# Prompt attention of a hybrid decoder step: where a step's products with the values stand in TensorE's order

## The reference, cut to what matters

```python
s = jnp.einsum('...qgrd,...kgd->...qgrk', q, k).astype(jnp.float32) * SCALE
p = jax.nn.softmax(jnp.where(mask, s, NEG), axis=-1)
o_win = jnp.einsum('...qgrk,...kgd->...qgrd', p.astype(v.dtype), v)   # o_sel, o_cmp alike
o = gates[..., 0:1] * o_cmp + gates[..., 1:2] * o_sel + gates[..., 2:3] * o_win
```

## Time and profile before

| | us |
|---|---|
| runs | 1827.85, 1829.54, 1830.10 (median 1829.54) |
| the profiled execution's own time | 1826.82 |
| its span, first to last instruction | 1825.2 |
| the attention stage's matmuls in it | from 648.3 to 948.5 |
| mean granted TensorE clock | 0.978 |

### The profile page before, as it was taken

The page is one execution under the profiler, slowest core; times in us unless marked ns, Lnnn a source line. Parts: engine busy times, 40 slices in busy tenths (PEclk is TensorE's granted clock), DMA queues, the critical chain, the costliest instruction groups (busy, mean ns, idle before and its releaser), DMA issues. The chain is left out here.

```text
span 1825.2 us, 29596 instructions
## 1 busy us (share of the span) xinstructions
PE 1713.0 (94%) x11664; PEld 1511.1 (83%) x11664; DVE 838.9 (46%) x1606; ACT 618.1 (34%) x1188; POOL 148.9 (8%) x261
## 2 busy tenths in 40 slices
PE   5999999995999779999989999999999999999997
PEld 4989988994864655555549889999999999999997
DVE  5556342131116366677775675322332233223476
ACT  5222322210010156666655554202320232023343
POOL 1000000013534300000000110000000000000011
PEclk9999999997999799999999999999999999999999
DMA  8111011144966500000017533211111111111365
GB/s 292 47 48 48 24 48 42 47 104 116 239 180 190 153 17 1 1 1 1 1 45 198 174 119 93 66 47 47 47 47 47 47 47 47 47 47 47 110 177 166
DMA packets 215500, 148.98 MB, mean 82 GB/s; under 512 B 13565, under 2 KB 204882, under 8 KB 214978
## 3 DMA queue, kind: packets, MB, share of 16 engines
q1 hardware_dynamic: 180050, 99.38, 19.4%
q0 software_dynamic: 12848, 37.47, 6.7%
q10 hardware_dynamic: 22464, 10.23, 2.2%
HBM read 134.76 MB, written 16.47 MB: 83 GB/s over the span
## 5 line engine op out<-in xcount | busy, mean ns | idle before, releaser
L2077 PE MATMUL psum<-act_hi,whi 128*128 128x344 f32 x960 | 310.2, 323 | 8.6 <-DVE wlo L2196 5.6
L2077 PE MATMUL psum<-act_lo,whi 128*128 128x344 f32 x960 | 307.4, 320 | 0.0
L2077 PE MATMUL psum<-act_hi,wlo 128*128 128x344 f32 x960 | 307.4, 320 | 0.0
L2196 DVE TENSOR_TENSOR wlo<-wraw,whi 128x1024 fp32r<-128x1024 f32 x111 | 136.0, 1225 | 253.7 <-ACT whi L2093 253.5
L2077 PE MATMUL psum<-hidden_hi,whi 128*128 128x344 f32 x768 | 246.4, 321 | 0.0
L2077 PE MATMUL psum<-hidden_hi,wlo 128*128 128x344 f32 x768 | 245.3, 319 | 0.0
L2077 PE MATMUL psum<-hidden_lo,whi 128*128 128x344 f32 x768 | 245.2, 319 | 0.0
L2093 ACT ACTIVATE whi<-wraw 128x1024 fp32r<-128x1024 f32 x111 | 117.4, 1057 | 338.1 <-PE psum L2077 332.0
L231 PE MATMUL psum<-act_hi,whi 128*128 128x344 f32 x648 | 214.8, 331 | 4.1 <-DVE act_lo L404 4.1
L231 PE MATMUL psum<-act_hi,wlo 128*128 128x344 f32 x648 | 208.1, 321 | 0.0
L231 PE MATMUL psum<-act_lo,whi 128*128 128x344 f32 x648 | 208.1, 321 | 0.0
(11 more groups left out here) (366 smaller groups left out, 2474.7 us busy)
## 6 DMA issues: line engine op xcount, KB each, us to landing
wraw<-in_w_down SPq DMA_DIRECT2D x48, 512.0 KB, 3.7
wraw<-in_w_up SPq DMA_DIRECT2D x40, 512.0 KB, 4.1
wraw<-in_w_in SPq DMA_DIRECT2D x27, 512.0 KB, 3.8
wraw<-in_w_o SPq DMA_DIRECT2D x23, 512.0 KB, 4.6
h_features<-mixed_then_h POOLq DMA_DIRECT2D x24, 172.0 KB, 2.5
h_again<-h_features POOLq DMA_DIRECT2D x24, 172.0 KB, 3.0
x_rows<-in_x_prompt SPq DMA_DIRECT2D x4, 1024.0 KB, 9.2
dec_pages<-in_cache_sel_k SPq DMA_DIRECT2D x64, 64.0 KB, 3.0
```

The lines of the kernel that those rows point to most:

```text
L2077: last = pe.matmul(ps[:, u % 3, 0:TN], wt[:, kt, :], xt[:, kt, cols], start=(kt == 0 and i == 0), stop=(kt == KT - 1 and i == 2))
L2196: dve.tensor_tensor(m.wlo[p % 2][:], wraw[raw_slot[p]][:], m.whi[p % 2][:].bitcast(F32), ALU.subtract).then_inc(lo_ready, 1)
```

## The change

In TensorE's loop `output` moves from the end of an iteration, behind `other_keys(k)`, to a place between `sel_keys(k)` and `turn(k-2)`, one iteration later: part x of a group is issued in the iteration after the one that had it before. The loop has one more iteration for it. On VectorE `add_halves` moves by one iteration too. No operation is added or left out, and ScalarE's list is untouched.

```diff
             pe.wait_ge(casts, 1)
-            for k in range(len(steps) + 6):
+            for k in range(len(steps) + 7):
                 if k < len(steps):
                     sel_keys(k)
+                if k >= R + 3:
+                    output((k - 3) // R - 1, (k - 3) % R)
                 if 2 <= k < len(steps) + 2:
                     turn(k - 2)
                 if k < len(steps):
                     other_keys(k)
-
-                if k >= R + 2:
-                    output((k - 2) // R - 1, (k - 2) % R)
@@ VectorE
-                if k % R == 2 and k >= 2 * R + 2:
+                if k % R == 3 and k >= 2 * R + 3:
                     add_halves(k // R - 2)
```

## The result

The changed kernel takes 1866.03 us (median of four runs, 1865.36 to 1867.41) against 1828.88 us before: a ratio of 1.0206, 95% interval [1.0193, 1.0219]. It is slower by 37 us. The profiled execution took 1865.63 us.

The account below looks back on a forecast made before the run. TensorE's own list was taken to bound the attention stage; 35.3 us of new waits for the selected exponential less 4.2 us of vanishing waits gave net +31 us on 1829.5, so 1860.5 us, range 1848 to 1873 (86%).

Parts of the forecast that it names:

- TensorE's list bounds the stage, and the products hide ScalarE's chain: Attention stage: TensorE's own work bounds it; 1.87 us of products cover ScalarE's copies and selected exponential, leaving 1.08 us spare.
- The sum of c - b, 35.3 us: Attention steps: c (first transpose to accumulator read plus 0.06) less b (to window scores' end), where positive: 35.3 us wait.
- What goes, 4.2 us: Attention stage: TensorE's existing waits for exponentials, mostly in the short steps at the end, vanish: 4.2 us taken off.
- Products followed by transposes cost the same as products followed by scores: TensorE's list in 56 attention steps: same 1.87 us price for eight instructions, with 6 us either way.
- I cost the clock at nothing: Attention stage: TensorE's granted clock stays at 1.00 throughout despite the new waits, adding 0 us.
- Nothing moves: Rival 1, TensorE's list: its work is the whole bound, so the exchange is free; 1829.5 us, 4%.
- Faster: Rival 2, attention stage: products cover VectorE's selected maximum, 4.2 us of waits vanish without a new one; 1825.3 us, 3%.
- VectorE's halves: Rival 3: query split and halves share an iteration, seven steps lose up to 2.1 us each; 1876 us, 5%.
- The falling clock: Rival 4, attention stage: a quarter of its 260 us at 1.2 GHz adds 65 us; some 1925 us, 2%.

Follow-up runs that it names:

- second comparison: The changed kernel run again without any edit, for a second profile: 1869.94 us, 1.0242 of the kernel before.
- only_after_r0: Kernel before, moving only the products that stood behind steps with r = 0 to behind the next step's selected scores: 1826.58 us, 1.0004.
- exp_first: Changed kernel with ScalarE's selected exponential of step k put ahead of the copies of step k-2: 1845.26 us, 1.0112 of the kernel before.
- vector_part_undone: Changed kernel with VectorE's add_halves put back at k % 4 = 2: 1872.33 us, 1.0244 of the kernel before.
- only_after_r123: Kernel before, moving only the products that stood behind steps with r = 1, 2, 3; those behind r = 0 stay: 1873.09 us, 1.0237.
- exp_before_last_copy: Changed kernel with ScalarE's selected exponential ahead of only the last copy of step k-2 and the compressed copy: 1835.11 us, 1.0037 of the kernel before.
- before_exp_first: Kernel before, products unmoved, with ScalarE's selected exponential put ahead of the copies of step k-2: 1891.44 us, 1.0344.
- between_turn_and_scores: Kernel before with the products moved behind the transposes, ahead of the same iteration's window scores: 1860.59 us, 1.0186.
- before_exp_before_last_copy: Kernel before, products unmoved, with ScalarE's selected exponential ahead of the last copy of the step two back: 1826.73 us, 0.9995.

## Why the prediction was right, and what it missed

The direction, the main mechanism and the range were right: 1866.0 us for 1860.5 (1848 to 1873). Against the median of before it is +37 us for +31, and +43 in the second comparison; in the profiled steps +42 for +31. The largest term was right, two terms put at nothing weren't.

- *TensorE's list bounds the stage, and the products hide ScalarE's chain.* Right. The run `only_after_r0` shows that a product costs nothing where the chain is hidden otherwise, and `exp_first` that the wait for the exponential disappears if it isn't behind the copies.
- *The sum of c - b, 35.3 us.* Measured waits: 32.4 us in 43 steps (the forecast says "some 42"; its own list by blocks counts 43). In step 11 the wait was 0.78 us for 0.85. The sum went by the distance between two starts, and a wait is counted from the end of the last matmul: from the start of the window scores to the next selected scores step 11 takes 1.92 us instead of 1.08, a difference of 0.84. With some 0.07 us more for each wait, the 32.4 us are about 35.5, just what was forecast.
- *What goes, 4.2 us.* Right that no wait for the window exponential is left, but 0.9 of the 4.2 us stood in front of step 6, which the move doesn't touch, and stayed. What went is 3.3 us. Net 32.4 - 3.3 = 29.1 us, and 13.0 of the 42.1 us are something else.
- *Products followed by transposes cost the same as products followed by scores.* This was a mis-sized term. The products themselves take 1.87 or 2.00 us as before, by the part. But the selected scores take 1.06 us up to the products instead of 0.99 up to the transposes (712.99 - 711.93), and the transposes behind the products some 0.05 us more. In a step with a wait that is 0.12 to 0.14 us, about 6 us in 43 steps; I had put it at 0, with 6 us either way. In the long steps with r = 0 it almost cancels, because the scores that stood ahead of the products are followed by other scores now and take less. Step 12 before and after (length, then the columns as above):

```profile
717.80:724.36 6.56, 6.31 (x42) 4.05 (x40) 4.21 (x9) 3.81 (x8) 0.00 (x0) 1.00 0.00 0
...
718.67:725.30 6.63, 6.38 (x41) 4.13 (x41) 4.08 (x9) 3.56 (x7) 0.00 (x0) 1.00 0.00 1
```

- *I cost the clock at nothing.* Wrong. Measured against the second profile, step 35 lost 1.3 us; against steps 60 and 61, which do the same work with two transposes fewer, steps 56 and 57 lost about 3.3 and 1.5. Together about 6 us. Of the 13.0 us this leaves some 7 for the switches and for the 0.07 us that each wait is counted short, which come to 9 by the figures above; the sum doesn't close to better than 2 us.
- *What sets off the drops isn't known.* Ahead of steps 55 and 56 TensorE stood still for 0.8 to 0.9 us, and step 55 has no products, but steps 41 to 51 have waits as long and ran at 1.00. All four profiles with the full waits (two of the changed kernel, `vector_part_undone`, `only_after_r123`) drop in step 56, the last two also in steps 60 and 61. In `exp_first` and `only_after_r0`, without these waits, and in `exp_before_last_copy`, with 7.6 us of them, no step from 6 to 62 was below 0.97. In those with the full waits, or with the waits for copies of `before_exp_first` and `between_turn_and_scores`, the time at 1.2 GHz came to 10 to 38 us. Three kernels stand between (`before_exp_before_last_copy` and the two with split transposes): 3 us each, in steps 52 and 53, with a wait of 1.1 us for the window exponential in step 52. That wait alone isn't the cause: the kernel before and `only_after_r0` have it and ran at 1.00. The longest times at the lower level come with the longest waits in total, but no run was made to single out a cause.
- *The rivals.* Nothing moves: excluded. Faster: excluded, for the reason given, the copies ahead of the exponential. VectorE's halves: excluded in the changed kernel by `vector_part_undone`, but by its trace on the path in `exp_first`. The falling clock: the fourth rival happened, in a small part of the stage, a tenth of the size it was given. The Trainium skill, "TensorE: Matmul & The Clock Gate", section "A second HAM failure mode: psum-queue depth-cycling", warned of this pattern, short idle times between groups with banks in turn. The trace agrees in part: the clock did fall in the stretch with such idle times, but only in three of 57 steps, and most steps with waits of up to 1 us ran at 1.00.

What I had seen only by half is what else the products cover. Where they stood, they hid two chains: the selected exponential, on which the prediction rests, and the window's maximum and exponential. `between_turn_and_scores` gave back the first cover and took the second, and was slower than the kernel before by 34 us.

## What to carry to other kernels

Before moving independent work in an engine's list, write down for each partner engine which of its instructions run during that work now, and what stands ahead of them in its own in-order list: here the work was covering an exponential that couldn't start earlier, only because copies were queued in front of it. Then look at the partner's order first; the cheap edit was to put the exponential ahead of the last copy. Moving a part alone, chosen where the time from the first transpose to the window scores' end is as long as the partner's chain, tests such a reading at once.

## What wasn't expected of the hardware

- The granted clock fell to the 1.2 GHz level in steps 6 to 62 of the changed kernel, in which TensorE never waited longer than 1.0 us for another engine, and in a stage in which it was busy for 86% of the time (287.4 of 335.1 us). The dip of steps 56 and 57 came at the same steps in two profiles of the same kernel, that of step 35 in one of them only. The cause is open.
- Going from the scores (128 weight columns) to the products (64 weight columns), and from these to the transposes, costs more than going from the scores straight to the transposes: 0.07 us on the scores' side and about 0.05 at the transposes (step 11). Whether the width of the weights is the reason wasn't tried.
